# A two-block transformer kernel: 64 seats for each expert instead of 128 for each expert group, with rounded rows and their rests stacked in one operand

## The chip, the cores and the metric

The kernel runs on 1 core of one Trainium2 chip. The metric is the device time of one execution in microseconds (us), lower is better. Three executions of the kernel before took 2308.28 to 2308.93 us, median 2308.36 us.

## What is computed

A first block (two layers of SwiGLU and mixed attention) is followed by a second block whose two layers each end in a mixture of experts. The change lies in that part alone:

```
def grouped_moe(x, w_router, b_router, w_gate, w_up, w_down):
    xt = x.reshape(B * S, D)                       # 256 tokens, D = 1024
    scores = softmax(xt @ w_router + b_router)     # 16 experts in 4 groups of 4
    grp = scores.reshape(-1, 4, 4)
    g_sel = argmax(sum of the two largest of each group)
    top_w, top_i = top_k(scores of the chosen group, 2); top_w /= sum(top_w)
    gate = the two weights at their experts, 0 elsewhere
    for e in range(16):
        h = silu(xt @ w_gate[e]) * (xt @ w_up[e])  # 1024 x 512 each
        y = y + gate[:, e:e + 1] * (h @ w_down[e]) # 512 x 1024
```

So each token takes part in one group and in two of its four experts. Computing the router of the reference for the inputs gives 47 to 86 tokens on a group and 17 to 55 on an expert in the two layers.

All values are float32. TensorE multiplies `fp32r` operands (rounded float32) in one pass, so an exact product is built from three: rounded x rounded, rounded x rest, and rest x rounded, where the rest is the value less its rounded part.

## The kernel before

**Weights.** SyncE streams all weights in chunks of 128 x 2048 floats (1 MB) into a ring (`load`, L507). In the expert stage the ring has six slots (`RINGS`), before it four. A load waits until TensorE has finished with the chunk that held the slot (`chunks_done`). ScalarE rounds a chunk into one of three buffers (`RH`, in `split`, L1565; it waits for the chunk three before) and VectorE subtracts, which leaves the rest in the slot itself (`RL`, L2065). TensorE then runs the three products (`split_products`, L675, with its matmuls at L687, L688 and L691).

**Expert stage.** Before it, VectorE works out the routing (L2645 to L2720): the best group of each token (`OH`), by two small matmuls its place within the group (L1384, L1385), and from the place a 0/1 matrix `SEAT` of 256 tokens x 128 seats for each group. TensorE gathers the tokens of a group into 128 columns with X as the stationary operand (`gather`, L1388, plain float32), ScalarE rounds them (L1965), VectorE makes the rest (L2756). In layer 0 the products of other chunks (`unit_ahead`) lie beside the routing; in layer 1 nothing does. If a group had over 128 tokens, a slower branch (`dense`) would run all experts on all tokens; the trace shows the other one.

An expert is six chunks: gate 0 and 1, up 0 and 1 (each K = 512 of the 1024 rows) and down 0 and 1. With 128 seats as the stationary operand each chunk is 4 x 3 matmuls of 512 columns. The order on TensorE (L1419 to L1450) is gate 0, four transposes of the hidden values of the expert before (L1361), gate 1, down 0 and 1 of the expert before, up 0, up 1. After the second expert of a group the next group is gathered. The hidden values pass ScalarE (silu L1941, rounding L1928) and VectorE (product with the gate weight L2738, rest L2746). The output of a group stays in PSUM over its four experts and is then copied (L1972, L2761); at the end `scatter` (L1415) brings the rows of all groups back to their tokens with `SEATT`, the transposed seats.

GpSimd runs little here: a few powers, and DMAs of the layer norm's vectors (L655).

## Time and profile before

| quantity | value |
|---|---|
| median of 3 runs | 2308.36 us |
| the profiled execution, span | 2304.4 us |
| TensorE matmul busy | 2264.1 us (98%) |
| VectorE busy | 1599.8 us (69%) |
| ScalarE busy | 1243.2 us (54%) |
| GpSimd busy | 48.1 us (2%) |
| bytes moved by DMA | 490.96 MB, mean 213 GB/s |

The profiled execution's span is 2304.4 us; what lies outside it (start and end of the program) is what separates it from the run times, 4.0 us against the median. Busy time of TensorE comes from modelled ends of pipelined matmuls: its share says that matmuls follow each other, not that each is as short as it can be. For a change in one stage the window of that stage counts: layer 0's experts run from about 1491 to 1786 us of the span, layer 1's from 1998 to 2294.

### The profile page before, as it was taken

How to read it: one execution, taken by the hardware profiler on the slowest of the kernel's cores; microseconds unless marked ns; L12 is line 12 of the kernel's file. 1: busy time of each engine (PE TensorE's matmuls, PEld its weight loads, DVE VectorE, ACT ScalarE, POOL GpSimd, SP SyncE). 2: the span in 40 equal slices, each digit the busy share in tenths (PEclk: the TensorE clock that was granted, in tenths of full speed). 3: DMA queues.
4: the chain of work that ended last, by engine and by line, in shares of the span. 5: the costliest groups of instructions: out<-in, count | busy, mean ns of one | idle time of the engine just before them, and what ended most of it. 6: DMA issues, size and time to landing. Idle time of an engine off the chain costs nothing.

```text
span 2304.4 us, 31674 instructions
## 1 busy us (share of the span) xinstructions
PE 2264.1 (98%) x13500; PEld 1969.0 (85%) x13500; DVE 1599.8 (69%) x1552; ACT 1243.2 (54%) x1272; POOL 48.1 (2%) x67
## 2 busy tenths in 40 slices
PE   8999999999999999999999999999999999899998
PEld 7888989788888899997888999888888998788886
DVE  6765755777477558556774656688887666688887
ACT  5444644444354346444443545577776545577775
POOL 1000100000000000000000000000000000000000
PEclk9999999999999999999999999999999999899999
DMA  8755453465555554445555554599997554599995
GB/s 249 208 189 176 131 163 126 161 189 187 185 181 183 189 160 143 152 140 171 186 194 190 170 171 165 184 341 346 370 345 277 179 183 148 197 346 345 346 369 186
DMA packets 309953, 490.96 MB, mean 213 GB/s; under 512 B 15504, under 2 KB 205120, under 8 KB 309808
## 3 DMA queue, kind: packets, MB, share of 16 engines
q1 hardware_dynamic: 305712, 475.35, 61.2%
q0 software_dynamic: 3104, 10.38, 1.6%
q10 hardware_dynamic: 992, 3.15, 0.4%
q8 instruction: 109, 1.79, 0.3%
q14 instruction: 36, 0.29, 0.0%
HBM read 487.40 MB, written 1.44 MB: 212 GB/s over the span
## 4 chain that ended last, share of the span: by engine, by line
PE 93%; DVE 4%; ACT 2%; issue 1%; DMA 0%; DVEq 0%; SPq 0%; ACTq 0%
PE PS L687 20%; PE PS L688 20%; PE PS L691 20%; PE PS L764 14%; PE PS L767 7%; PE PS L999 1%; PE PS L964 1%; PE PS L1396 1%; ACT RH L1565 1%; DVE RL L2065 1%; PE PS L938 1%; PE PS L949 1%; DVE X L2450 1%; PE PS L1361 1%; PE PS L1417 1%
## 5 line engine op out<-in xcount | busy, mean ns | idle before, releaser
L2065 DVE TENSOR_TENSOR RL<-RINGS,RH 128x2048 fp32r<-128x2048 f32 x448 | 1017.3, 2273 | 475.9 <-ACT RH L1565 473.4
L1565 ACT ACTIVATE RH<-RINGS 128x2048 fp32r<-128x2048 f32 x447 | 849.0, 1900 | 467.8 <-PE PS L691 449.1
L687 PE MATMUL PS<-RH,HTS 128*128 128x256 f32 (+1 forms) x1696 | 547.0, 334 | 1.0 <-DVE HTS L2756 0.5
L688 PE MATMUL PS<-RH,HTS 128*128 128x256 f32 (+1 forms) x1696 | 536.7, 328 | 0.0
L764 PE MATMUL PS<-HTS,RH 128*128 128x512 f32 x1384 | 415.0, 396 | 1.5 <-DVE HTS L2051 1.3
L691 PE MATMUL PS<-RL,HTS 128*128 128x256 f32 (+1 forms) x1696 | 400.0, 326 | 0.0
L687 PEld LDWEIGHTS PS<-RH,HTS 128*128 128x128 f32 x1696 | 319.3, 188 | 33.4 <-issue 2.5
L688 PEld LDWEIGHTS PS<-RH,HTS 128*128 128x128 f32 x1696 | 320.5, 189 | 28.0
L691 PEld LDWEIGHTS PS<-RL,HTS 128*128 128x128 f32 x1696 | 289.6, 189 | 31.2 <-DVE RL L2065 0.4
L764 PEld LDWEIGHTS PS<-HTS,RH 128*128 128x128 f32 x1384 | 248.0, 188 | 49.4 <-issue 1.7
L767 PE MATMUL PS<-HTS,RL 128*128 128x256 f32 x1408 | 283.2, 281 | 0.1
L767 PEld LDWEIGHTS PS<-HTS,RL 128*128 128x128 f32 x1408 | 228.7, 188 | 15.6 <-DVE RL L2065 0.5
L1579 ACT ACTIVATE Y<-PS 128x512 f32<-128x512 f32 x88 | 52.6, 597 | 231.3 <-PE PS L764 231.3
L687 PE MATMUL PS<-RH,GH 128*128 128x512 f32 x352 | 139.7, 397 | 0.0
L688 PE MATMUL PS<-RH,GL 128*128 128x512 f32 x352 | 137.8, 392 | 0.0
L688 PE MATMUL PS<-RH,EHL 128*128 128x512 f32 x256 | 100.5, 393 | 0.0
L687 PE MATMUL PS<-RH,EHH 128*128 128x512 f32 x256 | 100.4, 392 | 0.0
L691 PE MATMUL PS<-RL,GH 128*128 128x512 f32 x352 | 90.2, 391 | 0.0
L687 PEld LDWEIGHTS PS<-RH,GH 128*128 128x128 f32 x352 | 66.1, 188 | 16.2
L691 PEld LDWEIGHTS PS<-RL,GH 128*128 128x128 f32 x352 | 66.1, 188 | 15.0
L688 PEld LDWEIGHTS PS<-RH,GL 128*128 128x128 f32 x352 | 66.1, 188 | 14.6
L2096 DVE TENSOR_TENSOR Y<-PS,Y 128x512 f32<-128x512 f32 x44 | 30.4, 691 | 58.9 <-ACT Y L1579 58.6
(441 smaller groups left out, 2530.5 us busy)
## 6 DMA issues: line engine op xcount, KB each, us to landing
RINGS<-w_in SPq DMA_DIRECT2D x64, 1024.0 KB, 5.3
RINGS<-w_gate SPq DMA_DIRECT2D x64, 1024.0 KB, 5.4
RINGS<-w_up SPq DMA_DIRECT2D x64, 1024.0 KB, 5.5
RINGS<-w_down SPq DMA_DIRECT2D x64, 1024.0 KB, 5.2
RINGS<-ffn_w_up SPq DMA_DIRECT2D x44, 1024.0 KB, 5.3
RINGS<-ffn_w_down SPq DMA_DIRECT2D x44, 1024.0 KB, 4.9
RINGS<-ffn_w_gate SPq DMA_DIRECT2D x43, 1024.0 KB, 5.4
RINGS<-w_out SPq DMA_DIRECT2D x16, 1024.0 KB, 4.9
```

The source lines that it names most:

```text
L687: mm(dst, a_[0], b_[0], start=start, stop=False)
L688: mm(dst, a_[0], b_[1], start=False, stop=False) if left else mm(dst, a_[1], b_[0], start=False, stop=False)
L691: return mm(dst, a_[1], b_[0], start=False, stop=stop) if left else mm(dst, a_[0], b_[1], start=False, stop=stop)
L764: return mm(PS[:, bank + c, :], wh[:, k, c * P:(c + 1) * P], HTS[:, :, k, :], start=(k == 0), stop=(k == K - 1))
L767: mm(PS[:, bank + c, 0:S], wl[:, k, c * P:(c + 1) * P], HTH[:, k, :], start=False, stop=stop)
L938: last = mm(PS[:, 2 + g, j * nk:(j + 1) * nk], TT[hp:hp + 64, q, t * P:(t + 1) * P], TT[hp:hp + 64, kk, 0:nk], start=True, stop=True)
L949: last = nc.tensor.transpose(PS[:, 4 + i // 4, (i % 4) * P:(i % 4 + 1) * P], PRF[:, u % 2, i * P:(i + 1) * P], IDENT)
L964: last = mm(PS[:, 6, s_ * HD:(s_ + 1) * HD], PTF[:, u % 2, i * P:(i + 1) * P], PROJ[:, b, vc:vc + HD], start=(b == 0), stop=(b == t))
L1565: A(splits.buffer(RH, RH3)[:, 0:width], RINGS[:, slot, 0:width], ACT.Copy).then_inc(wh_ready, 1)
L1579: A(dst, PS[:, at:at + 2, S:2 * S], ACT.Copy).then_inc(part_copied, 1)
L2065: TTn(RL[:, slot, 0:width], RINGS[:, slot, 0:width], splits.buffer(RH, RH3)[:, 0:width].bitcast(F32), ALU.subtract).then_inc(wl_ready, 1)
L2096: link(TTn(hid, PS[:, bank + 2:bank + 4, 0:S], hid, ALU.add))
```

## The change

Each expert gets seats of its own, 64. The stationary operand of a gate or up matmul is now 64 columns of rounded rows beside the 64 columns of their rests (`XS`), so one pass with the rounded weights and one with the weights' rests give all products; the rests' part comes out in the other 64 rows of PSUM. ScalarE copies these other rows out and one more matmul with a swapping matrix (`folded`) adds them to the main rows. Even experts keep their result in rows 0 to 63, odd ones in 64 to 127. `selected` takes the place of the four transposes: it moves the 64 seats of the expert to the 128 seats of its group, so that down and `scatter` stay as they were. Down 0 and 1 of the expert before now come after up 1 on all engines, and in the order of the loads. The gather runs in `fp32r`, with X rounded by ScalarE (`rows_rounded`) and the rest of X by GpSimd (`XL`), over 256 seats of a group. The seats, their tables and the branch condition (over 64 tokens on an expert) are computed for 16 experts. Some semaphores are shared, which changes no order, and the comparisons of the routing are placed between dependent steps (`put`, `settle`). The diff, cut:

```diff
+SEATS = 64
...
+SEATG = over("SEATG", [P, NG_, T, P], at_proj + 16384)
+SEATX = [over(f"SEATX{g}", [P, T, EG * SEATS], at_pr + 2048 * g if g < 3 else at_kd + 8192) for g in range(NG_)]
+XH = over("XH", [P, T, D], at_pt)
+XL = [over(f"XL{t}", [P, D], at) for t, at in enumerate((at_zs, at_tt + 16384))]
+XS = HTS.rearrange("p a k n -> p (a k n)").rearrange("p (k j c) -> p k j c", k=K, j=EG)
+SWAP = over("SWAP", [P, P], at_pc)
...
+SEL = flat(BIAS)[:, 2 * D:2 * D + 1024].rearrange("p (i n) -> p i n", i=NE // 2)
+PICK = SMALL[:, 8:48].rearrange("p (t n) -> p t n", t=T)
+PLACE = SMALL[:, 48:88].rearrange("p (t n) -> p t n", t=T)
+OH = PICK[:, :, 0:NG_]
+GBANK = (1, 3, 6, 7)
+def main_rows(e):
+    return slice(64 * (e % 2), 64 * (e % 2) + 64)
+def other_rows(e):
+    return main_rows(e + 1)
...
                 for i in range(2):
                     src = a[n][l, e, i * 512:(i + 1) * 512, :].rearrange("(k p) n -> p k n", p=P)
                     load(src, lambda r: r.rearrange("p (k n) -> p k n", n=DE))
-                if n == "w_gate_2" and e:
-                    downs(e - 1)
+            if e:
+                downs(e - 1)
...
+            if k == 2:
+                for t in range(T):
+                    pool.wait_ge(xh_ready, T * l + t + 1)
+                    nc.gpsimd.tensor_tensor(XL[t], X[:, t, :], XH[:, t, :].bitcast(F32), ALU.subtract).then_inc(xl_ready, 1)
...
+        def stacked(bank, i, j):
+            slot = ring.next()
+            splits.n += 1
+            pe.wait_ge(wh_ready, splits.v + splits.n)
+            wh, wl = (w.rearrange("p (k n) -> p k n", n=DE) for w in (splits.buffer(RH, RH3), RL[:, slot, :]))
+            pe.wait_ge(wl_ready, splits.v + splits.n)
+            for k in range(4):
+                mm(PS[:, bank, :], XS[:, 4 * i + k, j, :], wh[:, k, :], start=(i + k == 0), stop=False)
+                last = mm(PS[:, bank, :], XS[:, 4 * i + k, j, :], wl[:, k, :], start=False, stop=(i == 1 and k == 3))
+            last.then_inc(chunks_done, 1)
+        def folded(bank, e, rests, count):
+            pe.wait_ge(rests_copied, 2 * (l * NE + e) + count)
+            mm(PS[:, bank, :], SWAP[other_rows(e), :], rests[other_rows(e), :], start=False, stop=True, skip_group_check=True).then_inc(fold_ready, 1)
+        def selected(e, bank):
+            pe.wait_ge(hid_rows, l * NE + e + 1)
+            for k in range(4):
+                last = mm(PS[:, bank, k * P:(k + 1) * P], EHID[main_rows(e), 0, k * P:(k + 1) * P], SEL[main_rows(e), e // 2, :], start=True, stop=True)
+            last.then_inc(hid_tr, 1)
...
-        both = OH.rearrange("p t g -> p (t g)")
-        mm(PS[:, 4, 32:40], CON[:, O_U:O_U + P], both, start=True, stop=True)
-        mm(PS[:, 4, 40:48], CON[:, O_ONE:O_ONE + P], both, start=True, stop=True).then_inc(pos_ready, 1)
+        both = PICK.rearrange("p t n -> p (t n)")
+        mm(PS[:, 4, 0:40], CON[:, O_U:O_U + P], both, start=True, stop=False)
+        mm(PS[:, 4, 0:20], CON[:, O_ONE:O_ONE + P], PICK[:, 1, :], start=False, stop=True)
+        mm(PS[:, 4, 40:80], CON[:, O_ONE:O_ONE + P], both, start=True, stop=True).then_inc(pos_ready, 1)
         if l == 0:
-            unit_ahead(13, 3)
+            unit_ahead(13, 2)
...
+            for b in range(4):
+                for k in (2 * b, 2 * b + 1):
+                    dst, at = PS[:, GBANK[b], (k % 2) * S:(k % 2 + 1) * S], slice(k * P, (k + 1) * P)
                     for t in range(T):
-                        last = mm(PS[:, 6 + i, k * P:(k + 1) * P], X[:, t, (4 * i + k) * P:(4 * i + k + 1) * P], SEAT[:, g, t, :],
-                                  start=(t == 0), stop=(t == T - 1))
+                        mm(dst, XH[:, t, at], SEATX[g][:, t, :], start=(t == 0), stop=False)
+                    for t in range(T):
+                        if g + k == 0:
+                            pe.wait_ge(xl_ready, T * l + t + 1)
+                        last = mm(dst, XL[t][:, at], SEATX[g][:, t, :], start=False, stop=(t == T - 1))
                 last.then_inc(gather_ready, 1)
...
+            def seat_tables():
+                pe.wait_ge(seat_ready, 2 * l + 2)
+                if l == 0:
+                    pe.wait_ge(unit_a, taken_at(1, 12)[1])
+                for i in range(NE // 2):
+                    for t in range(T):
+                        mm(PS[:, 4 + i // 4, i % 4 * P:(i % 4 + 1) * P], SEATX[i // 2][:, t, i % 2 * P:(i % 2 + 1) * P], SEATG[:, i // 2, t, :],
+                           start=(t == 0), stop=(t == T - 1))
+                for i in range(NE // 2):
+                    for t in range(T):
+                        mm(PS[:, 6, 2 * i:2 * i + 2], SEATX[i // 2][:, t, i % 2 * P:(i % 2 + 1) * P].bitcast(F32), GATE[:, 2 * i:2 * i + 2, t],
+                           start=(t == 0), stop=(t == T - 1))
+                for j in range(NG_):
+                    for t in range(T):
+                        last = nc.tensor.transpose(PS[:, 1 + j // 2 * 2, ((j % 2) * T + t) * P:((j % 2) * T + t + 1) * P],
+                                                   SEATG[:, j, t, :].bitcast(F32), IDENT)
+                last.then_inc(seat_tr, 1)
...
             for e in range(NE):
-                g, at = e // EG, (e // EG) % 2 * P
-                rows_in = [x[:, :, at:at + P] for x in HT]
-                if e % EG == 0:
-
-                    pe.wait_ge(seat_d, 2 * (l * NG_ + g) + (2 if e else 1))
+                g, j = e // EG, e % EG
+                if j == 0:
+                    pe.wait_ge(seat_d, 4 * (l * NG_ + g) + 2)
                 if e:
                     pe.wait_ge(gate_silu, l * NE + e)
-                gate_up(0, 0, rows_in, 1)
-                if e:
-                    hidden_transposed(e - 1, 1)
-                else:
-                    pe.wait_ge(seat_ready, l * NG_ + NG_)
...
-                gate_up(0, 1, rows_in, 1)
+                stacked(0, 0, j)
+                if j == 0:
+                    pe.wait_ge(seat_d, 4 * (l * NG_ + g) + 4)
+                stacked(0, 1, j)
                 if e == 1:
                     pe.wait_ge(seat_taken, l + 1)
-                if e > EG and e % EG == 1:
-                    pe.wait_ge(y_l, l * 5 + g)
                 if e:
-                    down(e - 1, (e - 1) % EG == 0, (e - 1) % EG == EG - 1, 1)
-                gate_up(2, 0, rows_in, 1)
-                gate_up(2, 1, rows_in, 1)
-                if e % EG == 1 and g < NG_ - 1:
-                    gather(g + 1)
+                    selected(e - 1, 7)
+                if l == 0 and e == 0:
+                    pe.wait_ge(unit_a, taken_at(1, 13)[1])
+                stacked(2, 0, j)
+                stacked(2, 1, j)
+                folded(0, e, CORG, 1)
+                if e == 0:
+                    seat_tables()
+                else:
+                    pe.wait_ge(eh_l, l * NE + e)
+                    if e > EG and j == 1:
+                        pe.wait_ge(y_l, l * 5 + g)
+                    down_part(0, (e - 1) % EG == 0, False, 1)
+                    if j == EG - 1 and g < NG_ - 1:
+                        gather(g + 1)
+                    down_part(1, False, (e - 1) % EG == EG - 1, 1)
+                folded(2, e, CORU, 2)
...
+        def rows_rounded(t):
+            act.wait_ge(x_rows, 2 * version(1, l, 2) + t + 1)
+            A(XH[:, t, :], X[:, t, :], ACT.Copy).then_inc(xh_ready, 1)
+        rows_rounded(0)
...
+            def rests(e, dst, bank):
+                A(dst[other_rows(e), :], PS[other_rows(e), bank, :], ACT.Copy).then_inc(rests_copied, 1)
+            def seated(e):
+                g, j = e // EG, e % EG
+                chunk()
+                split(back=3)
+                chunk()
+                rests(e, CORG, 0)
+                split(back=3)
+                if e:
+                    hidden_copy(e - 1, 7)
+                chunk()
+                split(back=3)
+                chunk()
+                rests(e, CORU, 2)
+                act.wait_ge(fold_ready, 2 * (l * NE + e) + 1)
+                A(ESIL[main_rows(e), 0, :], PS[main_rows(e), 0, :], ACT.Silu).then_inc(gate_silu, 1)
+                split(back=3)
+                if e == 0:
+                    seats()
+                    return
+                chunk()
+                split(back=3)
+                if j == EG - 1 and g < NG_ - 1:
+                    gathered(g + 1)
+                chunk()
+                if j == 0:
+                    group_rows(g - 1)
+                if e < NE - 1:
+                    split(back=3)
...
+        TTn(OH, eq, before, ALU.is_gt)
+        link(V.tensor_reduce(SMALL[:, 384:416], RTC2.rearrange("p (n j) -> p n j", j=4), AX.X, ALU.add))
+        for t in range(T):
+            last = V.scalar_tensor_tensor(PICK[:, t, NG_:NG_ + NE].rearrange("p (g i) -> p g i", i=4), SMALL[:, 384 + 16 * t:400 + 16 * t].rearrange("p (g i) -> p g i", i=4), 1.5,
+                                          spread(OH[:, t, :], 2, 4), ALU.is_lt, ALU.mult)
+        last.then_inc(oh_ready, 1)
...
+        link(TTn(PLACE, PS[:, 4, 0:40].rearrange("p (t n) -> p t n", t=T), PICK, ALU.mult))
+        def expert_seats(g):
+            for t in range(T):
+                last = TTn(SEATX[g][:, t, :].rearrange("p (j n) -> p j n", j=EG), spread(CON[:, O_NTH:O_NTH + SEATS], 1, EG),
+                           spread(PLACE[:, t, NG_ + EG * g:NG_ + EG * (g + 1)], 2, SEATS), ALU.is_equal)
+            return last
+        expert_seats(0).then_inc(seat_ready, 1)
...
+        gates()
+        for t in range(T):
+            TTn(SEATG[:, :, t, :], spread(CON[:, O_NTH:O_NTH + P], 1, NG_), spread(PLACE[:, t, 0:NG_], 2, P), ALU.is_equal)
         for g in range(1, NG_):
-            if g == 2:
-                gates()
-            seat(g, 1)
-            seat(g, 0).then_inc(seat_ready, 1)
+            last = expert_seats(g)
+        last.then_inc(seat_ready, 1)
...
+            def hidden(e):
+                dve.wait_ge(gate_silu, l * NE + e + 1)
+                dve.wait_ge(fold_ready, 2 * (l * NE + e) + 2)
+                V.scalar_tensor_tensor(EHID[main_rows(e), 0, :], PS[main_rows(e), 2, :], GSEAT[main_rows(e), e:e + 1], ESIL[main_rows(e), 0, :],
+                                       ALU.mult, ALU.mult).then_inc(hid_rows, 1)
+            def hidden_low(e, bank):
+                dve.wait_ge(eh_h, l * NE + e + 1)
+                TTn(EH[1][:, :, 0:P], PS[:, bank, :].rearrange("p (k n) -> p k n", k=4), EH[0][:, :, 0:P].bitcast(F32), ALU.subtract).then_inc(eh_l, 1)
+            def seated(e):
+                g, j = e // EG, e % EG
+                if e:
+                    hidden(e - 1)
+                split()
+                if e > EG and j == 1:
+                    group_rows(g - 1)
+                split()
+                if e:
+                    hidden_low(e - 1, 7)
+                    split()
+                    split()
+                split()
+                if j == EG - 1 and g < NG_ - 1:
+                    gathered(g + 1)
+                split()
+                ring.n += 6 if e else 4
```

## Rows read from the trace of the kernel before

**Rows 1.** The page, chain that ended last: shares by engine.
```profile
PE 93%; DVE 4%; ACT 2%; issue 1%; DMA 0%; DVEq 0%; SPq 0%; ACTq 0%
```

**Rows 2.** Layer 1, experts 1-15: us, busy PE, PEld, DVE, ACT, POOL; clock, DMA, GB/s.
```profile
2012.23:2279.54 267.31, 267.31 (x1237) 219.39 (x1236) 230.84 (x130) 193.23 (x129) 0.00 (x0) 1.00 0.95 345
```

**Rows 3.** Timeline of PE, one expert of layer 1: start us, us, engine, line, operation.
```profile
2052.80 0.60 PE L1361 MATMUL PS<-CON,Y 128*128 128x128 f32 x4
...
2069.91 0.60 PE L1361 MATMUL PS<-CON,Y 128*128 128x128 f32 x4
2070.26 0.47 PE L687 MATMUL PS<-RH,HTS 128*128 128x512 f32 x1
```

**Rows 4.** Timeline of PE, layer 0, products of one item of `unit_ahead`.
```profile
1478.71 0.28 PE L687 MATMUL PS<-MEMH,RH 128*128 128x256 f32 x1
1478.83 0.28 PE L688 MATMUL PS<-MEML,RH 128*128 128x256 f32 x1
1478.95 0.28 PE L691 MATMUL PS<-MEMH,RL 128*128 128x256 f32 x1
```

**Rows 5.** Groups by line and shape, 1500 to 1780 us: busy us, mean ns | idle before.
```profile
L2065 DVE TENSOR_TENSOR RL<-RINGS,RH 128x2048 fp32r<-128x2048 f32 x93 | 212.8, 2290 | 34.6 <-ACT RH L1565 33.5
L1565 ACT ACTIVATE RH<-RINGS 128x2048 fp32r<-128x2048 f32 x93 | 178.1, 1915 | 40.7 <-PE PS L691 40.6
...
L2738 DVE SCALAR_TENSOR_TENSOR Y<-PS,GSEAT,Y 128x512 f32<-128x512 f32 x16 | 11.9, 745 | 0.0
L1396 PE MATMUL PS<-PROJ,X 128*128 128x128 f32 x96 | 11.2, 275 | 0.0
...
L1928 ACT ACTIVATE EHH<-PS 128x512 fp32r<-128x512 f32 x16 | 9.6, 600 | 27.6 <-PE PS L1361 27.6
...
L2761 DVE TENSOR_TENSOR YS2L<-PS,YS2H 128x1024 fp32r<-128x1024 f32 x1 | 1.2, 1219 | 0.0
...
L1972 ACT ACTIVATE YS1H<-PS 128x1024 fp32r<-128x1024 f32 x1 | 1.0, 1028 | 0.8 <-PE PS L691 0.8
```

**Rows 6.** Loads issued closely in turn: the issues, and from issue to landing.
```profile
L518 SPq DMA_DIRECT2D RINGS<-w_gate x2: 505/506/507, 1488.3 to 1488.9; - x2
...
DMA to landing us min/median/max: 7.9/8.9/10.0
...
L518 SPq DMA_DIRECT2D RINGS<-w_down x1: 368/368/368, 1494.3 to 1494.3; - x1
...
DMA to landing us min/median/max: 7.1/7.1/7.1
...
L518 SPq DMA_DIRECT2D RINGS<-w_gate x2: 507/589/671, 1986.6 to 1987.3; - x2
...
DMA to landing us min/median/max: 7.8/9.1/10.3
```

**Rows 7.** The page, DMA issues: KB each, median us from issue to landing.
```profile
RINGS<-w_out SPq DMA_DIRECT2D x16, 1024.0 KB, 4.9
```

**Rows 8.** Timeline of PE, start of layer 1's experts.
```profile
1992.55 5.24 PE L1396 MATMUL PS<-PROJ,X 128*128 128x128 f32 x32 [1.18 <-DVE PROJ L2703]
1998.33 0.50 PE L687 MATMUL PS<-RH,HTS 128*128 128x512 f32 x1 [0.55 <-DVE HTS L2756]
...
2002.09 1.85 PE L1437 MATMUL PS<-GATE,PROJ 128*128 128x4 f32 x16
...
2012.23 0.39 PE L687 MATMUL PS<-RH,HTS 128*128 128x512 f32 x1
```

**Rows 9.** Timeline of DVE, rests of the first seats, layer 0 and layer 1.
```profile
1490.34 0.69 DVE L2756 TENSOR_TENSOR HTS<-PS,HTS 128x512 fp32r<-128x512 f32 x1 [1.99 <-ACT HTS L1965]
...
1997.59 0.68 DVE L2756 TENSOR_TENSOR HTS<-PS,HTS 128x512 fp32r<-128x512 f32 x1
```

**Rows 10.** Groups by line and shape, POOL.
```profile
L639 POOL TENSOR_TENSOR SMALL<-SMALL,NEGH 128x24 f32<-128x24 f32 (+1 forms) x4 | 12.9, 3218 | 91.9 <-DVE SMALL L2270 61.3 <-DVE SMALL L2287 30.6
...
L636 POOL MEMSET KD<- 128x1088 f32 x2 | 2.1, 1056 | 0.0
```

250 lines of the change are left out of this document (129 added, 121 removed).

## The prediction

> **What bounds it now.** I read the chain of waits on the page first: nearly all of the time it runs through TensorE, with almost no DMA in it [rows 1]. In the window of layer 1's experts 1 to 15 TensorE is busy throughout at the full granted clock, the DMA engines are busy for 0.95 of it at 345 GB/s, and VectorE for 231 of 267.3 us [rows 2]. So TensorE sets the pace, but loads and VectorE stand close behind it. That is what the reader is to see: work taken off TensorE is worth only the distance to the next limit. Layer 0's window looks the same, so I work out one layer and take it twice, apart from the start.
>
> The timeline of one expert gives 17.11 us from transposes to transposes, of which the transposes take 0.35 [rows 3]. The rest is 72 matmuls of 512 columns: 16.76 / 72 = 0.233 us each. Fifteen experts are 256.7 us and three gathers add 11.2 [rows 5], together 267.9 against 267.3 in the window: the account closes.
>
> **The steady expert, part by part.**
> - Gate and up: 48 matmuls become 32, 11.2 us become 7.5. The two folds add 2 x 0.233 = 0.5.
> - Using one stationary operand twice in turn: the first two products of an item share theirs and the third doesn't, and all follow at 0.12 us [rows 4]. I give the pairing nothing.
> - Transposes to `selected`: four plain float32 products of 128 columns. A gather has 16 of that kind in 11.2 / 3 = 3.73 us [rows 5], so 0.233 each and 0.93 against 0.35.
> - Down stays at 24 matmuls, 5.6 us.
> - TensorE's own sum is 7.5 + 0.5 + 0.9 + 5.6 = 14.5 instead of 17.1.
> - The gather: 32 products of 256 columns at the 0.12 of [rows 4] are 3.8, as before. Its four pieces instead of two cost ScalarE 4 x 0.60 and VectorE 4 x 0.68 [rows 5, 9].
> - VectorE: 6 x 2.29 + 0.75 + 0.68 = 15.2 [rows 5, 9], unchanged, but now above TensorE's sum.
> - ScalarE: 6 x 1.92 for rounding, 0.60 each for two copies of rests, silu and hidden rounding: 13.9 [rows 5].
>
> No engine's sum is the answer, because down now waits for a loop through three engines. From the start of gate 0: TensorE gate 0, 1.86; ScalarE then rounds up 1, copies the gate rests (by then gate 1 is done), rounds down 0 and rounds the hidden values, 1.92 + 0.60 + 1.92 + 0.60; VectorE makes the hidden rest and the rest of down 0, 0.68 + 2.29; TensorE runs down 0 and 1 and the last fold, 5.6 + 0.23. The sum is 15.7, and I take 15.8 for handing over. TensorE waits some 1.2 us of it before down 0, too little in my view to lose the clock. In place of TensorE the ordering of ScalarE and VectorE is what is late.
>
> A gather lies between down 0 and down 1 and adds its 3.8. A group's output copies (1.03 on ScalarE, 1.22 on VectorE [rows 5]) now lie ahead of the next up chunks; some 0.5 us of VectorE's idle time takes in part of the 2.25, and 1.8 are added. Both happen three times: 15 x 15.8 + 3 x 5.6 = 253.8.
>
> **The loads** decide how much of this comes true. Six chunks in 15.8 us want 2.63 us each. Where loads queue up, the landings are 1496.2, 1498.9, 1501.4 and 1994.4, 1997.6 [rows 6]: steps of 2.7, 2.5 and 3.2, mean 2.8. From above, the steady expert shows that 17.11 / 6 = 2.85 can be kept up [rows 3]; from below stands 2.5. At 2.8 the loads fall behind by 1.0 us in a plain expert and catch up in one with a gather or group copy. The tightest slot is down 1's: asked for when down 1 is done at 15.6, wanted for rounding 6.9 into the next expert, so 7 us, against 4.9 for a load alone [rows 7]. The 2.1 between takes in two plain experts' arrears; only the last three exceed it, and I add 0.5. Moving downs behind up in the queue costs nothing else. The stage is thus 254.3 instead of 267.3, **13.0 less per layer**.
>
> The Trainium skill (DMA: Bandwidth & Descriptors, Bandwidth) speaks of about 358 GB/s as a core's share of HBM when the pair streams, and of 425 measured for one core alone. The first would be 2.93 us a chunk and give about rival 1's time; the second, 2.47, would leave no arrears. The steady pace of [rows 3] is 6.29 MB in 17.11 us, 368 GB/s and so above the first; no row shows a long stretch faster than that.
>
> **The start of a layer.** The first expert took 13.9 us (1998.33 to 2012.23 [rows 8]). Now: 32 products 7.5, folds 0.5, and the tables: 16 for the selection (between 0.09, a transpose's 0.35 / 4, and 0.12: 1.9 taken), 16 with two columns, which cost 1.85 / 8 = 0.23 each [rows 8], so 3.7, and transposes 0.9. That is 14.5: **+0.6**.
> Ahead of it VectorE has more to do. In layer 1 nothing covers this: the places wait for the experts' picks and a third small matmul, 1.4 us (bounds: 0.6 if all of it lies in gaps, 2.2 if none). The seats after group 0 are six of 128x256 and two of 128x512 at 1.1 ns an element (2290 ns for 2048 [rows 5]) and an overhead of 0.07 each, 3.4 against 1.7 now. The rests of the first seats start at 1997.6 [rows 9] + 3.1, and two are wanted: 2002.1 instead of 1998.3, +3.8. GpSimd beside VectorE and a longer spell of lower clock get 0.6. **Layer 1: +5.0.** In layer 0 a chunk of matmuls covers the routing, but a second rest of weights now precedes the seats: 1.7 + 2.29 - 1.99 of idle time [rows 9] + 0.68 = 2.7, with the 0.6: **+3.3**.
> X rounded (ScalarE, about 1.03 each) fits before the transposes come and behind the exponential, 0.1. Its rest on GpSimd is not in the trace: at least the 1.06 of a fill of 1088 columns, at most the power's 3.2 us for 12 to 24 columns [rows 10], which would be some 180 us. A subtraction is nearer to the fill; I take 2.2, twice the fill since it reads two operands, and the gather of layer 1 comes some 4.6 us after the second tile is rounded, so it is hidden. The Trainium skill (GPSIMD Engine Reference, Elementwise) measures 4497 ns for 2048 elements, an estimate of 2.25 us.
> At the end `selected` again costs +0.6 a layer. All else there is as it was.
>
> **Sum:** 2 x 13.0 - 5.0 - 3.3 - 1.2 = 16.5 off the profiled span of 2304.4. The median of the runs is 4.0 above that span; I keep the distance: 2308.4 - 16.5 = **2292**. What a measurement of this kernel can tell from no change is about 0.2%, 4.6 us.
>
> **Rivals.**
> 1. *Loads keep a slower pace.* At 2.9 us a chunk, a little over the steady 2.85 and under the step of 3.2, the loads and not the loop set the stage: 15 x 17.4 = 261, and 260 with what the ring holds at its start. 2 x 7.3 - 9.5 = 5 off, **2304**, practically no change. For it: the 3.2 step and the DMA share of 0.95 [rows 2, 6]. Against it: 2.85 is kept for whole groups. Chance 0.14.
> 2. *VectorE is the only limit.* If queues smooth the loop out, the stage is 15 x 15.2 + 3 x (2.7 + 1.2) = 240: 2 x 27 - 9.5 = 45 off, **2264**. Against it: loads would have to land every 2.6 us, and ScalarE and VectorE run in order. Chance 0.08.
> 3. *Down's loads come late, slower than before.* The mechanism is the slot of down 1: with more loads outstanding a landing takes not 4.9 but 7.1 to 10.3 us [rows 6]. At 7.9 each expert waits 1 us in front of down 1, the stage is 269: the change loses 2 x 2 + 9.5 = 13, **2322**. It decides from about 7.5 us of mean landing, where the stage is 262.5 and both starts are just paid for. Against it: such landings are seen only where loads had just been held up. Chance 0.13.
> 4. *The change doesn't do what it says:* an expert with over 64 tokens would send a layer into the dense branch, 144 matmuls for each expert, 16 x 33.6 us = 538 instead of 290. The fullest expert has 55, so 0.01.
>
> **Chances.** Forecast 0.55 (2284 to 2300), rivals 0.14, 0.08, 0.13, 0.01; 0.09 for mixtures. Faster: 0.55 + 0.08 + 0.05 = 0.68. Same: rival 1 and some mixtures, 0.17. Slower: 0.15. The range runs from a stage of 251 with starts of half the price, 2280, to rival 1 with layer 1's start 4 us dearer, 2308.
>
> **What would show it.** In the profile after: gate 0 to gate 0 of a plain expert 15.7 to 16 us; about 1 us of TensorE waiting for VectorE's rest before the first down product; 19 to 20 us with a gather; the first gate product of layer 1's experts about 3.8 later against the end of routing; a window of experts 1 to 15 of about 254. The loop is wrong if TensorE waits elsewhere or VectorE has no idle time; the load account is wrong if ScalarE's roundings wait for DMA in many experts, or never. If the power row priced GpSimd, the gather would wait for it.

## The result, and the profile after

| | before | after |
|---|---|---|
| median of 4 runs | 2308.33 us (2308.28 to 2308.93) | 2291.03 us (2290.81 to 2292.04) |
| ratio | | 0.9926 (95% interval 0.9911 to 0.9940) |
| profiled span | 2304.4 us | 2289.0 us |
| experts 1 to 15, layer 0 / layer 1 | 267.4 / 267.3 | 248.7 / 249.15 |
| start of a layer's experts (first transposes of X to gate 0 of expert 1), change, layer 0 / 1 | | +8.2 / +9.8 |
| end of the last expert to layer 1's first transposes of X / to the end of the span, change | | +0.8 / +1.3 |

The forecast was 2292, and the time is 1 us below it. That is luck in good part: two of its terms were far off and cancelled. The stage gained 18.7 and 18.2 us instead of 13.0 each, and the starts lost 18.0 instead of 8.3. With 1.4 us lost ahead of layer 0's experts and 2.0 behind the two stages, 36.8 - 18.0 - 1.4 - 2.0 = 15.4, the difference of the spans.

The page of the kernel after, shares of the chain and landings of the experts' loads (KB each, median us from issue):
```profile
PE 89%; DVE 7%; ACT 2%; issue 1%; DMA 0%; DVEq 0%; SPq 0%; ACTq 0%
...
RINGS<-w_gate SPq DMA_DIRECT2D x64, 1024.0 KB, 7.6
RINGS<-w_up SPq DMA_DIRECT2D x64, 1024.0 KB, 8.0
RINGS<-w_down SPq DMA_DIRECT2D x64, 1024.0 KB, 7.5
```
Kernel after, windows; columns as in [rows 2]. The first is experts 1 to 15 of layer 1, the others are pieces of its start:
```profile
2013.71:2262.86 249.15, 245.24 (x1088) 185.75 (x1087) 230.68 (x135) 212.08 (x167) 0.00 (x0) 0.99 0.97 363
...
1984.00:1992.00 8.00, 5.30 (x24) 5.16 (x25) 6.09 (x29) 0.60 (x1) 0.26 (x1) 0.50 0.62 234
2008.00:2016.00 8.00, 8.00 (x37) 6.76 (x38) 2.25 (x3) 3.02 (x4) 0.00 (x0) 0.60 0.34 138
```
Against [rows 2] the stage is 18 us shorter with the same work on VectorE (230.7 and 230.8 us), and the DMA engines are taken for 0.97 of it. The last window is new: the granted clock is 0.60 where the seat tables are made, most of it at the lower level (1.2 GHz). The kernel before made its tables (2001 to 2004 us) at 1.00; its routing (1984 to 1992 us) stood at 0.71. Over the whole span the mean is 0.994 before and 0.990 after. From these and the two levels I estimate some 28 us at the lower level before and 46 after.

Kernel after, timeline of PE in one plain expert of layer 0, with what starts each part:
```profile
1535.58 1.16 PE L1433 MATMUL PS<-BIAS,Y 64*128 64x128 f32 x8
1536.67 0.50 PE L1420 MATMUL PS<-RH,HTS 128*128 128x512 f32 x1
1537.00 0.40 PE L1421 MATMUL PS<-RL,HTS 128*128 128x512 f32 x1
1537.24 0.40 PE L1420 MATMUL PS<-RH,HTS 128*128 128x512 f32 x1
...
1540.54 0.49 PE L1427 MATMUL PS<-CORG,SWAP 64*128 64x512 f32 x1
1540.96 0.50 PE L730 MATMUL PS<-RH,EHH 128*128 128x512 f32 x1
...
1542.90 1.09 PE L734 MATMUL PS<-RL,EHH 128*128 128x512 f32 x4
...
1546.68 0.50 PE L1427 MATMUL PS<-CORU,SWAP 64*128 64x512 f32 x1
1547.11 0.50 PE L1420 MATMUL PS<-RH,HTS 128*128 128x512 f32 x1
```
Read the starts, since the durations overlap. Gate 0 began at 1531.70. From start to start gate takes 3.88, `selected` 1.09, up 3.87, a fold 0.42, down 5.72 and the other fold 0.43, together 15.41. No idle time is shown in it, and none before down's first product. It answers to [rows 3], 17.11.

Kernel after, timeline of VectorE in the same expert (the bracket is idle time before and its releaser):
```profile
1533.02 0.76 DVE L2927 SCALAR_TENSOR_TENSOR Y<-PS,GSEAT,Y 64x512 f32<-64x512 f32 x1
1533.81 4.49 DVE L2202 TENSOR_TENSOR RL<-RINGS,RH 128x2048 fp32r<-128x2048 f32 x2
1539.05 0.69 DVE L2933 TENSOR_TENSOR EHL<-PS,EHH 128x512 fp32r<-128x512 f32 x1 [0.75 <-ACT EHH L2077]
1539.66 8.89 DVE L2202 TENSOR_TENSOR RL<-RINGS,RH 128x2048 fp32r<-128x2048 f32 x4
```
VectorE has 0.75 us of idle time in 15.41, so its own work is 14.66. Down 0's rest is the first of the four splits, ready at 1541.9: a microsecond after down 0 began, and a microsecond before the four products at 1542.90 that read it.

Kernel after, start of layer 1's experts on PE; it answers to [rows 8]:
```profile
1985.54 0.65 PE L1450 MATMUL PS<-SMALL,CON 128*128 128x40 f32 x2 [5.91 <-DVE SMALL L2842]
...
1995.98 0.50 PE L1420 MATMUL PS<-RH,HTS 128*128 128x512 f32 x1 [1.78 <-DVE HTS L2917]
...
2005.03 2.00 PE L1497 MATMUL PS<-SEATG,SEATX 128*128 128x128 f32 x16
2006.87 4.38 PE L1501 MATMUL PS<-GATE,SEATX 128*128 128x2 f32 x32
2011.11 1.95 PE L1505 MATMUL PS<-CON,SEATG 128*128 128x128 f32 x8
2012.99 0.79 PE L1427 MATMUL PS<-CORU,SWAP 64*128 64x512 f32 x1
2013.71 0.79 PE L1420 MATMUL PS<-RH,HTS 128*128 128x512 f32 x1
```
First product to gate 0 of expert 1: 17.73 against 13.90. The eight transposes take 1.88 (half the clock) and the two-column products 4.24.

Kernel after, VectorE and GpSimd in the routing of layer 1:
```profile
1976.93 3.10 DVE L2202 TENSOR_TENSOR RL<-RINGS,RH 128x2048 fp32r<-128x2048 f32 x1
...
1981.61 0.19 DVE L2804 TENSOR_TENSOR SMALL<-SMALL 128x24 f32<-128x24 f32 x1
...
1982.00 2.31 DVE L2809 TENSOR_TENSOR SMALL<-SMALL 128x24 f32<-128x24 f32 x1
```
```profile
1975.48 2.40 POOL L698 TENSOR_TENSOR XL<-X,XH 128x1024 fp32r<-128x1024 f32 x1
1981.86 2.39 POOL L698 TENSOR_TENSOR XL<-X,XH 128x1024 fp32r<-128x1024 f32 x1 [3.99 <-ACT XH L2009]
```
A small instruction of one shape takes 0.19 us at 1981.61 and 2.31 us at 1982.00. The second began 0.14 after GpSimd's subtraction and ended 0.06 after it. A split that met the other subtraction took 3.10 instead of 2.29. This is what I had priced at a part of 0.6.

### The profile page after: what moved, and what is told of

It is laid out like the page before. It is cut to its first block, busy times and chain, and to the rows that moved or that the text cites. A ratio compares the mean times of both kernels' runs of the same rounds, so it can differ in the third digit from the quotient of the medians.

```text
span 2289.0 us, 31322 instructions
## 1 busy us (share of the span) xinstructions
PE 2232.0 (98%) x13248; PEld 1911.4 (84%) x13248; DVE 1612.9 (70%) x1576; ACT 1292.0 (56%) x1360; POOL 57.9 (3%) x71
## 3 DMA queue, kind: packets, MB, share of 16 engines
q0 software_dynamic: 3104, 10.38, 1.6%
q8 instruction: 107, 1.75, 0.3%
## 4 chain that ended last, share of the span: by engine, by line
PE 89%; DVE 7%; ACT 2%; issue 1%; DMA 0%; DVEq 0%; SPq 0%; ACTq 0%
PE PS L730 15%; PE PS L731 15%; PE PS L734 14%; PE PS L807 14%; PE PS L810 7%; PE PS L1420 5%; PE PS L1421 4%; DVE RL L2202 2%; ACT RH L1661 2%; PE PS L1433 1%; PE PS L1042 1%; PE PS L1007 1%; PE PS L1427 1%; PE PS L981 1%; PE PS L992 1%
## 5 line engine op out<-in xcount | busy, mean ns | idle before, releaser
L730 PE MATMUL PS<-RH,HTS 128*128 128x256 f32 (+1 forms) x1184 | 342.6, 305 | 0.4 <-DVE HTS L2184 0.4
L731 PE MATMUL PS<-RH,HTS 128*128 128x256 f32 (+1 forms) x1184 | 336.2, 300 | 0.0
L734 PE MATMUL PS<-RL,HTS 128*128 128x256 f32 (+1 forms) x1184 | 260.9, 298 | 0.0
L810 PEld LDWEIGHTS PS<-HTS,RL 128*128 128x128 f32 x1408 | 228.8, 188 | 15.7 <-DVE RL L2202 0.5
L730 PEld LDWEIGHTS PS<-RH,HTS 128*128 128x128 f32 x1184 | 224.1, 189 | 11.9 <-issue 2.5
L731 PEld LDWEIGHTS PS<-RH,HTS 128*128 128x128 f32 x1184 | 225.0, 190 | 7.3
L1420 PE MATMUL PS<-RH,HTS 128*128 128x512 f32 x512 | 210.7, 411 | 13.1 <-DVE RL L2202 8.3
L1421 PE MATMUL PS<-RL,HTS 128*128 128x512 f32 x512 | 203.0, 396 | 0.0
L1420 PEld LDWEIGHTS PS<-RH,HTS 128*128 128x128 f32 x512 | 97.7, 191 | 49.2 <-issue 24.4
L1421 PEld LDWEIGHTS PS<-RL,HTS 128*128 128x128 f32 x512 | 97.8, 191 | 18.7
```

The costliest lines, as they stand in the source:

```text
L730: mm(dst, a_[0], b_[0], start=start, stop=False)
L731: mm(dst, a_[0], b_[1], start=False, stop=False) if left else mm(dst, a_[1], b_[0], start=False, stop=False)
L734: return mm(dst, a_[1], b_[0], start=False, stop=stop) if left else mm(dst, a_[0], b_[1], start=False, stop=stop)
L810: mm(PS[:, bank + c, 0:S], wl[:, k, c * P:(c + 1) * P], HTH[:, k, :], start=False, stop=stop)
L1420: mm(PS[:, bank, :], XS[:, 4 * i + k, j, :], wh[:, k, :], start=(i + k == 0), stop=False)
L1421: last = mm(PS[:, bank, :], XS[:, 4 * i + k, j, :], wl[:, k, :], start=False, stop=(i == 1 and k == 3))
```

## The experiments

All start from the kernel after, whose time is 2291.03. The medians, in us:

| | median | lowest to highest | ratio to before, 95% interval |
|---|---|---|---|
| e1 one input on GpSimd | 2285.96 | 2284.80 to 2293.96 | 0.9902 to 0.9931 |
| e2 rests on VectorE | 2291.19 | 2286.90 to 2292.40 | 0.9908 to 0.9935 |
| e3 tables mixed | 2292.17 | 2290.84 to 2296.24 | 0.9918 to 0.9945 |
| e4 rests behind | 2284.81 | 2283.77 to 2287.42 | 0.9880 to 0.9910 |
| e5 light gates | 2285.97 | 2284.74 to 2287.46 | 0.9887 to 0.9917 |
| e6 rounded later | 2290.52 | 2288.49 to 2292.81 | 0.9907 to 0.9934 |
| e7 rest waited for first | 2315.12 | 2312.44 to 2318.82 | 1.0017 to 1.0041 |
| e8 fewer products | 2279.54 | 2278.75 to 2281.83 | 0.9863 to 0.9893 |
| e9 filled | 2290.87 | 2290.38 to 2293.94 | 0.9915 to 0.9942 |
| e10 combined | 2279.11 | 2278.22 to 2280.44 | 0.9857 to 0.9887 |
| e11 combined and filled | 2276.44 | 2275.73 to 2276.84 | 0.9847 to 0.9877 |
| e12 e11 with fewer products | 2272.48 | 2271.46 to 2273.36 | 0.9827 to 0.9860 |

The runs of one kernel spread up to 9 us (the kernel before: 1.6), because the stretches of half clock fall in different places from run to run: e1's three runs at 2285 to 2286 have a mean granted clock of 0.992, its two at 2292 to 2294 have 0.987 and 0.988. Where an edit is worth 1 to 3 us I read its stretch in the trace and not the median. A trace is one run, too. Seat tables that no edit touches take 6.69 to 9.52 us in layer 1 in the traces of e1, e2, e4, e6, e7, e8 and e9, and 7.96 in the kernel after, so differences of 1 to 2 us in them show nothing.

### e7: was down's wait in the loop?

```diff
 def down_part(i, first, end, tiles):
+    pe.wait_ge(wl_ready, splits.v + splits.n + 1)
     add_rows(4, EH, 2 * i, first and i == 0, end and i == 1, tiles)
```


> Against 2291.0. TensorE waits for the rests of down's weights before down's first product instead of before its last four: the wait that my walk through the engines had in it. Theory A (my walk, 15.7 to 15.8 from gate 0 to gate 0, was right but for this one place): the plain expert becomes 15.7 to 15.8, 2299 to 2302. Theory B (the trace of the changed kernel: gate 0 at 0, ScalarE's hidden values at 7.35, VectorE's hidden rest 0.69 and split 2.25 to 10.3, then down 5.6 and the fold 0.43): 16.2 to 16.4, about 0.9 more in each of 28 experts, 2312 to 2318. Theory C (the wait is covered, VectorE is ahead of it): 15.4, 2291.

Theory B: 2315.12, and plain experts of 16.44 to 16.56. The timeline of VectorE and of PE in one (its gate 0 began at 2043.63):
```profile
2051.04 0.69 DVE L2934 TENSOR_TENSOR EHL<-PS,EHH 128x512 fp32r<-128x512 f32 x1 [0.87 <-ACT EHH L2078]
2051.64 6.68 DVE L2203 TENSOR_TENSOR RL<-RINGS,RH 128x2048 fp32r<-128x2048 f32 x3
```
```profile
2052.51 0.50 PE L1428 MATMUL PS<-CORG,SWAP 64*128 64x512 f32 x1
2054.03 0.47 PE L730 MATMUL PS<-RH,EHH 128*128 128x512 f32 x1 [1.02 <-issue]
...
2059.76 0.49 PE L1428 MATMUL PS<-CORU,SWAP 64*128 64x512 f32 x1
2060.18 0.51 PE L1421 MATMUL PS<-RH,HTS 128*128 128x512 f32 x1
```
Here is the wait of about 1 us that I had forecast for the changed kernel: 1.02 before down 0. The view names "issue" for it; the first of VectorE's three splits ends at about 2053.9, just before down 0 begins. So the loop exists once the wait is put there. It is 0.8 longer than I walked it: the hidden rest begins 7.4 after gate 0 and not 6.9, down begins at 10.4 and not 9.9, and down with its fold takes 6.15 instead of 5.8. In the changed kernel the wait stands before down's last four products, and the loop closes with time to spare. Theory A's form of the walk (15.7 to 15.8) falls as well.

### e8 and e12: what is the next limit?

Every second product with a weights' rest in gate and up is left out, in the kernel after (e8) and in the best one (e12).
```diff
 for k in range(4):
     mm(PS[:, bank, :], XS[:, 4 * i + k, j, :], wh[:, k, :], ...)
-    last = mm(PS[:, bank, :], XS[:, 4 * i + k, j, :], wl[:, k, :], ...)
+    if k % 2:
+        last = mm(PS[:, bank, :], XS[:, 4 * i + k, j, :], wl[:, k, :], ...)
```


> Against 2291.0. In gate and up every second product with the weights' rests is left out (8 of 48 matmuls of an expert; half of the rests' share is missing from the result); loads, roundings and copies stay. TensorE has 1.84 us less an expert. Theory A (TensorE sets the pace, VectorE with 6 splits, 0.76 and 0.69 is next at 14.66): the plain expert goes from 15.41 to 14.7 to 14.9 and VectorE has no idle time left, the expert with a gather from 19.14 to 17.3, the one with a group's copies little; 11 to 13 us a layer, 2265 to 2270. Theory B (the six loads set the pace, 2.57 us each): 15.4 stays, only the experts with a gather gain; 2285 to 2290. Theory C (my walk through ScalarE and VectorE is the pace): a walk with 0.46 less in gate 0 alone, 14.9 to 15.0.

None of the three theories gave the time: 2279.54. From expert 0's last fold to expert 15's the stage takes 243.7 and 245.2 us instead of 249.0 and 249.4, a gain of 5.2 and 4.2 for 27.6 us less of products. e8, layer 1's experts, groups by line, and then a piece of ScalarE's timeline:
```profile
L1662 ACT ACTIVATE RH<-RINGS 128x2048 fp32r<-128x2048 f32 x89 | 170.4, 1915 | 28.5 <-DMA RINGS<-w_up 10.1 <-PE PS L734 7.4 <-DMA RINGS<-w_gate 6.3
L1420 PE MATMUL PS<-RH,HTS 128*128 128x512 f32 x240 | 80.3, 416 | 21.8 <-DVE RL L2203 20.1 <-ACT RH L1662 1.1
```
```profile
2084.77 1.92 ACT L1662 ACTIVATE RH<-RINGS 128x2048 fp32r<-128x2048 f32 x1 [0.43 <-DMA RINGS<-w_gate]
2087.48 1.92 ACT L1662 ACTIVATE RH<-RINGS 128x2048 fp32r<-128x2048 f32 x1 [0.79 <-DMA RINGS<-w_up]
2090.17 1.91 ACT L1662 ACTIVATE RH<-RINGS 128x2048 fp32r<-128x2048 f32 x1 [0.78 <-DMA RINGS<-w_up]
```
Where ScalarE waits for DMA, chunks arrive 2.71 and 2.69 us apart. TensorE is shown as waiting for VectorE's rests (20.1 us), but VectorE waits for ScalarE's roundings, and these wait for loads (16.4 us): the releaser that a view names is only the last link. e12 tells loads from the order of the rests:

> The kernel of e11 (2276.4 us), with every second product with the weights' rests left out in gate and up (half of the rests' share is missing from the result): 1.84 us less TensorE an expert. From the end of expert 0's last fold to the end of expert 15's the kernels with rests behind and e8 took 245.2 to 246.5 us, with 0.99 of the DMA engines' time taken and 90 chunks, 2.72 us each, though e8 had 27 us less of products. Theory A (the loads are the limit at 2.7 us a chunk, and the stages of 245 to 246 already stand on it): 243 to 246 again, 2273 to 2277. Theory B (e8 was held by the order of the wait for the rests, which the rests behind remove; VectorE's 14.66 us and 2.5 with a gather, 1.25 with copies, set the pace): 15 x 14.7 + 3 x 3.7 = 232, 2248 to 2255.

2272.48. The stages take 241.2 and 244.9 us, so Theory A's size stands (one layer is 2 below its interval, the time 0.5) and B's 232 does not. Experts with a gather show it best: with 1.84 us less of products than in e11 they take 19.35 to 21.80 us, against 19.23 to 19.51. Windows of e8 and e12 in layer 1:
```profile
2006.00:2250.80 244.80, 223.02 (x966) 161.39 (x966) 230.35 (x135) 212.34 (x167) 0.00 (x0) 1.00 0.99 369
```
```profile
2003.00:2243.00 240.00, 225.35 (x955) 159.76 (x954) 226.18 (x132) 209.41 (x164) 0.00 (x0) 0.99 1.01 376
```
In neither is VectorE or ScalarE full, though VectorE comes near (226 of 240 us), and the DMA engines are. The rate of the DMA engines in 40 slices of 5.5 us, e8, 2020 to 2240 us:
```profile
GB/s 404 391 387 407 388 387 297 357 392 404 391 386 406 389 387 406 388 389 268 336 394 403 391 387 401 394 384 404 390 386 319 319 395 401 395 385 403 392 387 405
```
Between the dips a load lands each 2.7 us (386 to 407 GB/s). The three dips are the gathers. A gather lies between down 0 and down 1, so once down 0's slot is free no other comes free for 6.6 us. In the kernel after, a load is issued at 2058.38 and the next at 2064.94; only one other is then in flight, and it lands in 4.99 us. With the dips the mean is 376 GB/s in e12's window and 369 in e8's, which takes in a slack start and end: 2.79 and 2.84 us a load. The stage uses 90 chunks in 241.2 to 245.2 us, 2.68 to 2.72 us each, because the ring holds some at its start; 86 to 88 land inside it. So the floor under this stage is the loads as this ring and this place of the gathers let them be issued, and the kernel after stands 2 to 3% above it. No run moved a gather or changed the number of slots, so how much of it is the rate itself is not shown. The Trainium skill (DMA: Bandwidth & Descriptors, Bandwidth) gives about 358 GB/s when both cores of the pair stream and 425 for one alone with 16 MB; the windows lie between, with one core at work and loads of 1 MB.

### e4: the stationary operand in turn, and waiting for the rests

```diff
-    pe.wait_ge(wl_ready, splits.v + splits.n)
     for k in range(4):
         mm(PS[:, bank, :], XS[:, 4 * i + k, j, :], wh[:, k, :], ...)
+    pe.wait_ge(wl_ready, splits.v + splits.n)
+    for k in range(4):
         last = mm(PS[:, bank, :], XS[:, 4 * i + k, j, :], wl[:, k, :], ...)
```


> Against 2291.0. In the stacked chunks the four products with rounded weights come first, then the wait for the weights' rests and the four products with them, instead of in turn with one stationary operand for each pair. Theory A (of my prediction: sharing a stationary operand in turn is worth nothing, the pitch is 0.230 us either way; TensorE sets the pace of an expert): the pitch stays 0.230, the plain expert 15.4; the first chunk starts on the rounded weights 0.5 to 2 us earlier at the start of each layer, and expert 0 waits less between its chunks (0.83 now): 2288 to 2291. Theory B (the shared stationary operand saves a load of weights each time): 16 more weight loads an expert that show, some 0.03 to 0.06 us each, 0.5 to 1 us an expert: 2305 to 2320.

2284.81, below the range of either theory. The plain expert takes 15.45 instead of 15.41, so the operand used twice in turn is worth 0.04 an expert: nothing, as forecast. What was missing in Theory A is the expert behind a group's output copies: 15.92 instead of 16.89, three times a layer. Timelines of PE of the kernel after and of e4 in such an expert (layer 0), all rows with an idle time:
```profile
1590.33 0.47 PE L1420 MATMUL PS<-RH,HTS 128*128 128x512 f32 x1 [1.25 <-DVE RL L2202]
```
```profile
1591.04 1.20 PE L1422 MATMUL PS<-RL,HTS 128*128 128x512 f32 x4 [0.18 <-DVE RL L2203]
```
TensorE waited 1.25 for the rest, now 0.18. The pairing itself forces the wait for the rest to the front of each chunk. Where VectorE is behind, that costs; the form of down, which waits before its last four, doesn't.

### e1, e2, e6: GpSimd's subtraction and VectorE

e1 gives GpSimd one input (XH times zero, so the rests of X are left out of the result); e2 gives the subtraction to VectorE and takes it from GpSimd; e6 moves ScalarE's rounding behind the next split. Their edits, in this order:
```diff
-nc.gpsimd.tensor_tensor(XL[t], X[:, t, :], XH[:, t, :].bitcast(F32), ALU.subtract)
+nc.gpsimd.tensor_scalar(XL[t], XH[:, t, :].bitcast(F32), 0.0, 0.0, ALU.mult, ALU.add)
```
```diff
+for t in range(T):
+    dve.wait_ge(xh_ready, T * l + t + 1)
+    TTn(XL[t], X[:, t, :], XH[:, t, :].bitcast(F32), ALU.subtract).then_inc(xl_ready, 1)
 dve.wait_ge(oh_ready, l + 1)
 dve.wait_ge(pos_ready, l + 1)
```
```diff
-rows_rounded(1)
 if l == 0:
     ahead.experts = ahead.n
     split(back=3)
+    rows_rounded(1)
     chunk()
     take_ahead(12, 5)
 split(back=3)
+if l:
+    rows_rounded(1)
```


> Against the changed kernel's 2291.0 us. GpSimd's two subtractions of the rows' rests in each layer become instructions of the same size with one input (XH times zero), so that the rests of the gathered rows are left out. Theory A (a VectorE instruction with two inputs in SBUF is held while GpSimd's instruction with two inputs runs): the VectorE line of 128x24 that took 2.31 and 2.35 us takes 0.17 to 0.21, the split of weights beside the other subtraction 2.29 instead of 3.10; from the transposes of X to the matmul of the places in layer 1 some 3 us less (14.45 becomes about 11.4), in layer 0 up to 2; in all 2286 to 2288. Theory B (any long GpSimd instruction on SBUF holds VectorE, whatever its inputs): the same two lines stay at 2 us or more, less only by what GpSimd's instruction is shorter; 2290 to 2291. Theory C (the long line was chance and the start is late by VectorE's added work alone): the line is short in some layers only, and the time stays at 2291.

> Against 2291.0. VectorE makes the rests of the rows itself, both layers, between the experts' picks and its wait for the places; GpSimd does nothing there. Theory A (GpSimd holds VectorE for 3.0 us in layer 1 and some 2.2 in layer 0): the hold goes, VectorE gets 2 x 1.15 = 2.3 us of work, of which 1.66 us lie in its wait for the places in layer 1: layer 1 gains 3.0 - 0.6 = 2.4, layer 0 gains 0 to 1 (there VectorE has no wait at that place, 2.2 against 2.3); 2287.5 to 2288.7. Theory B (no hold, the work is only moved): layer 1 loses 0.6, layer 0 loses 2.3; 2293 to 2294.

> Against 2291.0. ScalarE rounds the second half of the rows one split of weights later (1.9 us), so that GpSimd's second subtraction begins when VectorE's row of small routing instructions is over or nearly so; nothing is added or left out. Theory A (a VectorE instruction with two inputs in SBUF waits for the end of GpSimd's): no routing instruction of 128x24 at 2.3 us; from the router's first matmul to the places' last in layer 1 11.62 becomes 9.3 to 9.6 (it was 9.49 with GpSimd's one-input instruction), in layer 0 10.6 becomes 10.0 to 10.1; a split of weights beside it is held 0.8 in layer 0; 2288 to 2289.5. Theory B (GpSimd's instruction at a later time holds something else just as long, the first seats for one): 2290.5 to 2292.

e1, VectorE and GpSimd in layer 1:
```profile
1979.63 0.95 DVE L2809 TENSOR_TENSOR SMALL<-SMALL 128x24 f32<-128x24 f32 x1
...
1980.64 0.17 DVE L2809 TENSOR_TENSOR SMALL<-SMALL 128x16 f32<-128x16 f32 x1
```
```profile
1979.49 1.05 POOL L698 TENSOR_SCALAR XL<-XH 128x1024 fp32r<-128x1024 f32 x1 [4.50 <-ACT XH L2009]
```
Theory A said 0.17 to 0.21 for that line and is wrong there: with one input GpSimd still holds it, to its own end (1980.54 and 1980.58), only for a shorter time. Theory B is right on the mechanism, and wrong on what it is worth: router to places in layer 1 went from 11.62 to 9.49 us.

e2, without GpSimd:
```profile
1982.30 0.19 DVE L2805 TENSOR_TENSOR SMALL<-SMALL 128x24 f32<-128x24 f32 x1
...
1983.62 2.35 DVE L2857 TENSOR_TENSOR XL<-X,XH 128x1024 fp32r<-128x1024 f32 x2
```
The hold is gone, and router to places takes 8.72. The gather starts 0.5 later after that, as does the first product, so layer 1 gains 2.4 here, Theory A's number. The median shows none of it: in this trace the block of tables met the half clock in full (19.22 us from the first product to expert 1, against 17.73), and layer 0's stage took 1.3 us more. e6, layer 1:
```profile
1983.63 0.19 DVE L2811 TENSOR_TENSOR SMALL<-SMALL 128x24 f32<-128x24 f32 x1
...
1986.93 1.31 DVE L2867 TENSOR_TENSOR SEATX<-CON,SMALL 128x256 fp32r<-128x256 f32 x2
```
Router to places 9.56, and then the first seats, with two inputs in SBUF too, are held for 0.55. Both theories have their part; the total, 2290.52, can't be told from 2291.03. The hold moves with the subtraction and lasts as long as it meets such an instruction. The Trainium skill (SBUF — State Buffer, Who interferes with whom) states the rule: a VectorE instruction with two SBUF inputs and a GpSimd instruction that reads SBUF exclude one another for a whole instruction, whichever begins first. The traces agree, down to e1's one-input instruction and to what is not held: the rests of X, with one input in PSUM, keep 0.62 us each beside GpSimd's subtraction in the kernel after.

### e3, e5, e9: the tables and the clock

> Against 2291.0. The same instructions of the seat tables in another order: the 16 matmuls of two columns go between the 16 of 128 columns and the eight transposes, pair by pair, instead of in a block. Theory A (the block of two-column matmuls, in which TensorE does little, is what the granted clock falls after): the granted clock stays above 0.9 behind the tables, the transposes take 0.9 instead of 1.88 us, the first fold and expert 1 lose their extra 1.6 to 1.8; 2.5 to 3 us a layer, 2285 to 2286.5. Theory B (the clock falls because of the waits of TensorE ahead of the experts and the tables' work as a whole; its order does nothing): 2290.5 to 2291.5, with the same stretch at 0.5. Between them, a fall that comes later or is shorter: 2287 to 2290.

e3 puts each pair's two-column products between its selection products and the transposes. 2292.17, a little above Theory B's range and far from A's, and 8.8 us from the tables' first product to the next fold in layer 0 (7.66 in the kernel after). This order gains nothing that can be seen.

```diff
-mm(PS[:, 6, 2 * i:2 * i + 2], SEATX[...].bitcast(F32), GATE[:, 2 * i:2 * i + 2, t], ...)
+mm(PS[:, 6, 4 * i:4 * i + 4], SEATX[...], GATEP[:, t, 4 * i:4 * i + 4], ...)
...
+link(V.tensor_copy(parts[:, :, :, 0], GATE))
+TTn(parts[:, :, :, 1], GATE, parts[:, :, :, 0].bitcast(F32), ALU.subtract)
```


> Against the changed kernel's 2291.0 us. The gates of the seats are gathered by 16 matmuls of four rounded columns (gate rounded, gate's rest) in place of 16 matmuls in full fp32 of two columns, which took 3.94 and 4.24 us, 0.25 each; VectorE makes the two parts (two small instructions and two hand-overs, some 0.6 us) and adds them on the way out. Theory A (these matmuls are dear because they are full fp32, and the stretch of half clock behind them is as long as they are slow): a block of 1 to 1.5 us, 2.7 less a layer, and the half clock costs 0.5 to 1 less in the fold and expert 1; first product of the experts to gate 0 of expert 1 in layer 1 17.73 becomes 14.5 to 15; VectorE's additions give back 0.5 in layer 1: 2283.5 to 2286. Theory B (the block's time is hidden, because what ends expert 0 is VectorE's and ScalarE's rounding of the next weights): 17.73 stays above 17, 2289.5 to 2291.5.

Theory A: 2285.97. e5, layer 1:
```profile
2006.50 1.89 PE L1502 MATMUL PS<-GATEP,SEATX 128*128 128x4 f32 x16
2008.25 1.54 PE L1506 MATMUL PS<-CON,SEATG 128*128 128x128 f32 x8
```
The block takes 1.75 us instead of 4.24, and first product to expert 1 14.84 instead of 17.73. In layer 0 that is 15.73 instead of 18.16. Both lie below every trace with the old block and all products (16.46 to 19.22). VectorE's two instructions cost 0.46 in each.

e9 fills TensorE's waits with products that nobody reads (20 behind the router in layer 1, 6 behind each first gather):
```diff
+for k in range(20):
+    mm(PS[:, 0, :], HTH[:, k % K, 0:P], HTS[:, :, k % K, :], start=True, stop=True)
```


> Against the changed kernel's 2291.0 us. TensorE makes products that nobody reads, into bank 0, where it has nothing to do: 20 of 512 columns (4.6 us at full clock) in layer 1 while it waits 5.9 us for the experts' picks, and 6 (1.4 us) behind the first gather in both layers, where it waits 1.8 and 2.7. Theory A (the granted clock falls because TensorE stands idle there, and rises again when it has work): in layer 1 the places' matmuls and the gather run at full clock, the gather's first ten pairs at 0.23 instead of 0.43, so 2 us of gather and 0.5 of places less; the stretch of half clock at 1498 to 1501 in layer 0 goes as well, 0.5 to 1; 2286.5 to 2288.5. Theory B (the clock falls whatever TensorE does, and the products only stretch over what follows): 20 products at half clock are 8.6 us, layer 1 is 2 to 3 later; 2293 to 2296.

2290.87, no difference. In layer 1 each theory has its part. The places' products now run at the full clock (0.24 us apart instead of 0.43), and router to first product is 20.60 instead of 21.19. But the half clock then takes in the tables: from start to start the two-column block is 5.43 us in this trace, where it was 4.24, and first product to expert 1 is 18.92. That the filling caused this is not shown: without it the same block took 5.73 us in e2 and 5.80 in e4.

### e10, e11: together

> Three edits that keep the whole computation, together: rests behind the rounded products (alone 2284.8), the light gates (alone 2286.0) and the later rounding of the rows' second half (alone 2290.5). Theory A (they are worth their parts, since they lie in different places: group copies and first chunks 6.2, tables 5.0, routing 0.5 to 2): 2278 to 2281. Theory B (what the light tables give is taken by the wait for the next weights once the first chunks start earlier; the loads are near their limit): 2282 to 2285.

> The three edits and the products that nobody reads, 13 (3.0 us) in the shorter wait of layer 1 and 6 behind the first gather of each layer. Theory A of the filled kernel gives 2 to 4 less than the combined one, 2275 to 2279. Theory B gives 1 to 3 more, 2280 to 2286.

e10 (rests behind, light gates, later rounding) takes 2279.11: the parts add up, Theory A. e11 adds the products that nobody reads (13 and 6) and takes 2276.44, 2.7 less, and no run of one reaches a run of the other. Where it comes from is in the traces. Windows of e10 and then of e11, the start of layer 0's first expert:
```profile
1496.00:1504.00 8.00, 6.13 (x16) 4.88 (x17) 5.48 (x7) 2.62 (x2) 0.00 (x0) 0.57 0.74 253
1496.00:1504.00 8.00, 6.26 (x27) 5.15 (x28) 7.14 (x7) 4.58 (x4) 0.00 (x0) 1.00 0.94 334
```
With the six products behind the first gather, expert 0's 32 products take 7.62 us instead of 10.04, at a granted clock of 1.00 instead of 0.57. Another 1.2 lies in layer 1's stage. In layer 1 the start gains nothing (37.32 us from the transposes of X to expert 1, against 37.04). The mean clock is 0.993 in all four runs of e11 and 0.989 to 0.991 in those of e10. The half clock meets expert 0 in layer 0 in some kernels without filling (e4: 10.38 us) and not in others (e5: 8.61, with a wait in it), so the filling seems to keep it away there; whether the light tables have a part in the gain, no run tells.

Both kernels compute all that the reference asks. e11 is 14.6 us below the kernel after and 32 below the one before; its stage in layer 1 is 246.1 us, nearly the loads' floor.

## Why the prediction came out, step by step

- **TensorE's own sum, 14.5: wrong, 15.41.** 0.230 a product was right. Missing were some 0.1 at each change to another chunk or kind (0.6 in all), 0.16 of `selected`, and the folds: 0.42 to 0.43 each from start to start, not 0.233.
- **VectorE's sum, 15.2: wrong, 14.66.** 2.29 is the duration shown; in a row a split takes 2.22 (8.89 for four). So VectorE is not above TensorE.
- **The loop, 15.8: wrong, and the step that failed first.** I had down 0 wait for its rest at its first product. The code waits before the last four, and e7 shows what the other would be: 16.5. TensorE, not the order of ScalarE and VectorE, still sets the pace. 15.8 was near 15.4 for a wrong reason, by luck, and cost 3.1 us of eight plain experts.
- **Gather, 3.8: right** (3.73). **Group copies, 1.8: mis-sized**, 1.48, or 2.1 us with the base of three experts.
- **Loads, 2.8 us a chunk: size and part right.** They land each 2.7 us between gathers, 2.79 in the mean of e12's window. Six at 2.7 take 16.2 in a plain expert of 15.41, which runs up arrears that gathers pay back. The 0.5 for it was about nothing. Of the signs, ScalarE's roundings do wait for DMA, but little: 6.2 us for up chunks in layer 1's stage and 2.2 in layer 0's. Rival 1's 2.9 falls. So do the 358 GB/s of the Trainium skill (DMA: Bandwidth & Descriptors, Bandwidth) as a bound for this core: the stage's window has 363.
- **Rival 3** had its condition met (medians of 7.5 to 8.0 us to landing) and not its price. With several loads in flight and one landing mostly each 2.6 to 2.8 us, 7.5 is queue, not delay: a load that is issued early waits behind others, and one issued behind a gather, with one other in flight, lands in 4.99.
- **The stage:** too dear by 3.1 + 1.0 (gathers' bases) + 2.1 + 0.5, too cheap by 1.4 (expert 1 runs partly at half clock, 17.24): 254.3 against 249.0 from fold to fold.
- **The starts, 8.3: the term mis-sized most, 18.0.** In layer 1 (9.8) the places came 3.5 later, of which 2.1 to 2.9 is GpSimd holding VectorE (e1, e2): I named GpSimd beside VectorE as a part of 0.6, and looked at whether its own time was hidden and not at whom it holds. From the places to the first product 2.5, most of it VectorE's seats. The first expert +3.8 and not +0.6: tables at 7.96 instead of 6.5, a wait of 0.83 between chunks, and the last fold at half clock. Layer 0 has the same block, +4.2, and 3.9 ahead of it, where 2.7 and 0.6 had been forecast.
- **Ends +0.6 each:** 0.94 in each layer from the end of the stage to the last scatter products; with what lies behind them 0.8 and 1.3. **Ahead of the experts:** 1.4 that I had no term for, in code that the change leaves alone. The first transposes of X come 1.4 to 2.9 us later in the traces of the kernel after and all twelve edits than in the one trace of the kernel before, so it is hardly chance. Between 200 and 600 us the granted clock is 0.99 in the kernel after and 1.00 in the one before; what brings that about is open.

What stays open: what sets the stretches of half clock, in time. In e9 (places of layer 1) and e11 (expert 0 of layer 0) the clock is full where TensorE had work in place of idle time; these are single traces, with e11's mean clock in all its runs behind one of them. e3 tried one other order of the tables, and it moved nothing for the better.

## What to carry to other kernels

Before a walk through several engines is believed, look up at which product each wait stands in the code: one line (e7) is worth 24 us here. A step between two chunks also holds back the loads that wait for the second one's slot, as the gathers do here. When work goes to GpSimd, ask not only whether it is hidden, but which VectorE instructions with two SBUF inputs run beside it. When products share a stationary operand, the wait for the later of the two moved operands comes first; share it only where both are ready.

## What was not expected of the hardware

- A VectorE instruction of 0.19 us is shown with 2.31 us when it begins just after GpSimd's 2.4 us one: the hold is inside the duration and no idle time points to it. A one-input instruction on GpSimd (1.05 us) holds it too.
- Rounded products of four columns cost 0.11 us each and full float32 ones of two columns 0.25, both measured partly at half clock.
- Products whose result nobody reads gained 2.7 us in e11, most of it in layer 0's first expert, and nothing in e9.
- One core keeps 376 GB/s of 1 MB loads for 240 us (e12, DMA share 1.01): one each 2.7 us between gathers, one each 2.79 with them.
